# The memory's key and value units alternate between two PSUM banks, and every fourth step VectorE makes the turned weights' low halves ahead of the row maxima

## The reference, cut to what matters

```python
# differential attention, 4 heads, query blocks of 128, causal
s1 = jnp.einsum('bhqd,bhkd->bhqk', qblk[:, :, 0], k1)
s2 = jnp.einsum('bhqd,bhkd->bhqk', qblk[:, :, 1], k2)
p1 = jax.nn.softmax(jnp.where(causal, s1, NEG_INF), axis=-1)
p2 = jax.nn.softmax(jnp.where(causal, s2, NEG_INF), axis=-1)
w = p1 - lam32 * p2
out = jnp.einsum('bhqk,bhkd->bhqd', w, vh)
...
attn = rms_norm(attn, subln[i]) * (1.0 - lam_init)
...
# cross attention: the keys and values of the memory
kv = (mem_n @ wkv).reshape(b, m, 2, N_CROSS_HEADS, CROSS_HEAD_DIM)
```

## Time and profile before

| what | value |
|---|---|
| median of 3 runs | 2087.31 us |
| the profiled execution's own time | 2086.56 us |
| its span, first to last instruction | 2084.8 us |
| mean granted TensorE clock | 0.998 |
| TensorE busy | 2068.5 us (99%) |
| VectorE busy | 1651.4 us (79%) |
| ScalarE busy | 983.4 us (47%) |
| attention loop, layer 0 | from about 471 to 558 us of the span |
| attention loop, layer 1 | the same, some 1028.4 us later |

### The profile page before, as it was taken

The page is one execution under the profiler, slowest core; times in us unless marked ns, Lnnn a source line. Parts: engine busy times, 40 slices in busy tenths (PEclk is TensorE's granted clock), DMA queues, the critical chain, the costliest instruction groups (busy, mean ns, idle before and its releaser), DMA issues.

```text
span 2084.8 us, 35632 instructions
## 1 busy us (share of the span) xinstructions
PE 2068.5 (99%) x14647; PEld 1915.8 (92%) x14647; DVE 1651.4 (79%) x2459; ACT 983.4 (47%) x1483; POOL 149.1 (7%) x112
## 2 busy tenths in 40 slices
PE   9999999999999999999999999999999999999998
PEld 7999998889888889999989999988888888999997
DVE  7998886659754889988799988766696457898885
ACT  6444444446533544444454444443464345444442
POOL 0000003100120300000110000030002111000001
PEclk9999999999999999999999999999999999999999
DMA  6333323323331343433233333243233224333321
GB/s 198 102 112 106 100 85 120 119 81 102 102 102 41 98 125 107 124 95 91 80 113 118 107 114 104 66 144 99 81 103 111 71 69 133 91 112 103 102 85 56
DMA packets 268028, 212.32 MB, mean 102 GB/s; under 512 B 7422, under 2 KB 234332, under 8 KB 267868
## 3 DMA queue, kind: packets, MB, share of 16 engines
q1 hardware_dynamic: 264608, 205.55, 31.7%
q10 hardware_dynamic: 3260, 4.51, 0.8%
HBM read 207.93 MB, written 2.10 MB: 101 GB/s over the span
## 4 chain that ended last, share of the span: by engine, by line
PE 93%; DVE 5%; ACT 2%; issue 0%; ACTq 0%; DVEq 0%
PE ps L2116 18%; PE ps L1989 13%; PE ps L1991 13%; PE ps L1990 13%; PE ps L2217 11%; PE ps L2216 11%; PE ps L2218 11%; DVE nb L1837 1%; DVE w_lo L1193 1%; ACT ex L1075 1%; DVE ex L1857 1%; DVE ps L1835 0%; PE ps L2367 0%; PE ps L2558 0%; PE ps L2003 0%
## 5 line engine op out<-in xcount | busy, mean ns | idle before, releaser
L2116 PE MATMUL ps<-hid_hi,wn_hi 128*128 128x256 f32 x1088 | 212.0, 276 | 0.0
L2116 PE MATMUL ps<-hid_hi,wn_lo 128*128 128x256 f32 x1088 | 211.8, 276 | 0.0
L2116 PE MATMUL ps<-hid_lo,wn_hi 128*128 128x256 f32 x1088 | 211.8, 276 | 0.0
L1452 DVE SCALAR_TENSOR_TENSOR h<-ps,h 128x512 f32<-128x512 f32 x224 | 152.7, 683 | 30.3 <-PE ps L2116 26.8
L663 ACT ACTIVATE w_hi<-raw 128x2048 fp32r<-128x2048 f32 x61 | 117.0, 1918 | 123.0 <-PE ps L1991 90.9
L2116 PEld LDWEIGHTS ps<-hid_hi,wn_hi 128*128 128x128 f32 x1088 | 163.9, 188 | 0.0
L2116 PEld LDWEIGHTS ps<-hid_hi,wn_lo 128*128 128x128 f32 x1088 | 163.7, 188 | 0.0
L2116 PEld LDWEIGHTS ps<-hid_lo,wn_hi 128*128 128x128 f32 x1088 | 163.7, 188 | 0.0
L2216 PE MATMUL ps<-hn_hi,form_hi 128*128 128x256 f32 x576 | 159.0, 276 | 0.0
L2218 PE MATMUL ps<-hn_hi,form_lo 128*128 128x256 f32 x576 | 159.0, 276 | 0.0
L2217 PE MATMUL ps<-hn_lo,form_hi 128*128 128x256 f32 x576 | 159.0, 276 | 0.0
(11 more groups left out here) (339 smaller groups left out, 6122.3 us busy)
## 6 DMA issues: line engine op xcount, KB each, us to landing
sraw<-in_ffn_wgu_dram SPq DMA_DIRECT2D x144, 512.0 KB, 4.9
raw<-in_ffn_wd_dram SPq DMA_DIRECT2D x48, 512.0 KB, 3.8
raw<-in_ffn_wd_dram SPq DMA_DIRECT2D x80, 256.0 KB, 4.0
raw<-in_w_in_dram SPq DMA_DIRECT2D x40, 512.0 KB, 4.5
raw<-in_cross_wkv_dram SPq DMA_DIRECT2D x32, 512.0 KB, 4.3
raw<-in_ffn_wgu_dram SPq DMA_DIRECT2D x30, 512.0 KB, 4.8
raw<-in_w_out_dram SPq DMA_DIRECT2D x16, 512.0 KB, 4.2
raw<-in_cross_wq_dram SPq DMA_DIRECT2D x16, 512.0 KB, 3.8
```

The costliest lines, as they stand in the source:

```text
L1452: dve.scalar_tensor_tensor(out=h[:, m, :], in0=ps[:, down_bank(c, m), :], scalar=0.5, in1=h[:, m, :], op0=ALU.mult, op1=ALU.add).then_inc( ...
L2116: last = pe.matmul(ps[:, bank, c], w, src[:, b, c], start=opens, stop=stop and n == 2, skip_group_check=half == 1)
```

## The change

`kv_bank` becomes one function for all engines and puts units 2, 4 and 6 into bank 3, next to `head_norm`. TensorE's waits follow: unit n from 3 on waits for the low half of unit n - 2 (for unit 3 of unit 0), unit 2 for the last of the value tiles that was in bank 3, units 4 and 6 also for ACT's copy of bank 3 for head 0 and head 1. `head_norm` part 1 waits for the low half of the unit that was in bank 3 before it. On DVE `turned_low(s - 1)` moves ahead of `maxima(s)` at s = 3, 7, 11 and 15; the other steps keep their order.

```diff
+        def kv_bank(n):
+            return 1 if n == 1 else 3 if n in (2, 4, 6) else 2
+
...
-                def kv_bank(n):
-                    return 1 if n == 1 else 2
...
+                    if s < 16 and s % 4 == 3:
+                        turned_low(s - 1)
                     if s < 16:
                         maxima(s)
                     if s == 0:
                         gate_chunk(3)
-                    if 2 <= s < 17 and s % 4 != 1:
+                    if 2 <= s < 17 and s % 2 == 0:
                         turned_low(s - 1)
...
                 if part == 1:
                     pe.wait_ge(osq_ready, L * 4 + hd + 1)
+                    pe.wait_ge(kv_ready, L * 8 + min(2 * hd + 3, 8))
...
                 def cross_kv(s):
                     n, c = s // 2, s % 2
                     if c == 0:
                         wait_unit(L, CK + n)
-                        if n >= 2:
-                            pe.wait_ge(kv_ready, L * 8 + (1 if n == 2 else n))
+                        if n >= 3:
+                            pe.wait_ge(kv_ready, L * 8 + (1 if n == 3 else n - 1))
                         else:
                             pe.wait_ge(v_ready, L * 4 + kv_bank(n) + 1)
+                        if n in (4, 6):
+                            pe.wait_ge(orb_ready, L * 4 + n // 2 - 1)
```

## The result

The changed kernel takes **2102.61 us** (median of six runs, 2098.10 to 2105.88) against 2087.34 for the kernel before (six runs, 2087.25 to 2087.45): ratio 1.0069, 95% interval 1.0059 to 1.0079. It is slower, as forecast, but by 15.3 us and not by 8.6, and its time lies above the range. The spread matters too: 7.8 us from run to run, where the kernel before had 0.2 in its six runs here and up to 2.7 in the 21 runs beside each group of experiments.

What follows compares the result with a forecast made beforehand. TensorE held 93% of the chain, but DVE and ACT set the pace in the attention loops' ring. Two layers at 4.3 us added 8.6 to the profiled 2086.56, the median 0.75 more: 2095.9 us, range 2089.9 to 2098.7.

Steps and rivals of the forecast that it cites:

- Part 1: DVE's reorder at steps 3, 7, 11 and 15: maxima and exponentials come 0.33 us later each time.
- Part 2: Units 4 and 6 in bank 3 wait for ACT's late copy; with the reorders, 4.3 us more per layer.
- Part 3: The other edits, including unit 2, unit 3, head_norm and new wait instructions: put at nothing, at worst 1.2 us for the instructions.
- the 2.57: Delay of unit 4's start, 509.31 instead of 506.74, with the first 0.33 us reorder included.
- the stands: TensorE standing still before units 4 and 6, waiting for ACT's copy: some 2.8 us, four times in all.
- rival 3: Slower still, 5%: clock falls to 1.2 GHz after each stall, four times 2.8, 11.2 us more, 2107 us.
- the lower bound: If DVE made up its delay between the copies: 2.57 + 0.33 a layer, 5.8 in all, 2093.1 us.
- The 0.88 of the earlier trace: Granted clock, of 2.4 GHz, in the 7 us at the kernel's end where TensorE runs out of work.
- Rivals 1 and 2: First, 4%: waits go, nothing replaces them, 2084.4 us. Second, 6%: stall off the path, only reorders count, 2089.9 us.

Runs made afterwards that it cites:

- order_only: Kernel before with only VectorE's new order (turned_low ahead of maxima), banks and waits as before: 2090.07 us, ratio 1.0015.
- copy_early: Changed kernel with ACT's copy of bank 3 ahead of its 1.93 us rounding of a weight unit: 2090.04 us, ratio 1.0014.
- copy_late: Changed kernel with ACT's copy of bank 3 one place later, behind the exponentials of the next step: 2109.52 us, ratio 1.0104.
- bank_copy_early: Changed kernel with VectorE's old order and ACT's copy of bank 3 ahead of its weight-unit rounding: 2087.55 us, ratio 0.9999.
- again: Changed kernel run once more with no edit: 2101.51 us, ratio 1.0066.
- bank_only: Kernel before with only the change's banks and their waits, VectorE's order as before: 2097.42 us, ratio 1.0054.
- wait_only: Kernel before with one added wait, units 4 and 6 for ACT's copy, though they stay in bank 2: 2100.07 us, ratio 1.0053.
- low_late: bank_copy_early with VectorE making the step's weights before the unit's low half: 2084.89 us, ratio 0.9986.
- low_late_old_banks: low_late without the exchange of banks, all units except 1 in bank 2 with the waits of before: 2086.77 us, ratio 0.9998.

## Why the prediction was right in part, and wrong in its time

**Part 1, the reorder, held.** 0.33 us in each of steps 3, 7, 11 and 15 was forecast; order_only measures 1.35 us a layer. At step 3 the score of step 5 starts at 489.26 - 1.81 (the late start) = 487.45; 487.43 was forecast.

**Part 2, the wait for ACT's copy, held.** Unit 4 starts at 511.17 - 1.81 = 509.36; the forecast was 509.31. The forecast of 4.3 us a layer stands against some 4.45 at full clock, worked out from the loops. Bank 3's later reader is ACT's copy, and copy_early and copy_late move the cost down and up with it alone. Part 3, nothing for the other edits, is borne out by bank_copy_early at 2087.55. One slip in the bounds changes nothing: behind the 2.57 two reorders are left in a layer, 0.66 and not 0.33, so the lower bound would be 2093.8 and not 2093.1.

**What failed is a term of the sum put at nothing: the clock behind the stands.** The prediction worked out the length of the stand, 2.8 us, and named the fall of the clock as rival 3, but gave it 5%, since "no row here shows one", and let TensorE run at full clock behind it. In the four profiles that have a gap of 2.66 to 2.91 us the clock fell at 13 of 16 places (three of four here, four in again, two in bank_only, four in wait_only), and after a gap of 4.21 us at four of four. One fall cost 515.59 - 511.17 - 2.80 = 1.62 us in the first place, 1.64 between the two layers and 1.64 in bank_only; where the slow stretch lasted about twice as long, it cost 2.79, which is the price that rival 3 put down for each. Three falls of the short kind are some 5 us, and two layers at 4.45 make 8.9: 2087.3 + 13.9 = 2101.2, inside the measured spread and 1.4 below the median, whose own rows are not known. The profile's remaining 1.8 are the start.

The row that rival 3 draws on was also read too coarsely. The 0.88 of the earlier trace rows is a mean of the two levels: in the kernel before the clock is full up to 2075 and at 1.2 GHz behind that, up to the end of the span.

```profile
2073.00:2075.00 2.00, 2.00 (x21) 2.00 (x19) 0.11 (x1) 0.00 (x0) 0.00 (x0) 1.00 0.00 0
2075.40:2077.40 2.00, 1.62 (x8) 1.22 (x7) 0.43 (x2) 0.28 (x1) 1.02 (x1) 0.50 0.00 0
```

TensorE was still at work when it fell: it had waited 0.85 us for VectorE before the transposes at 2072.76 (a gap of 1.12 from start to start), and had then made transposes and sixteen matmuls of one column each. So the trace of before held a fall behind a wait much shorter than 2.8 us. The work around it is unlike that of the loop, so it gave no chance for the four stands; but it was no reason for as little as 5%.

The page "TensorE: Matmul & The Clock Gate" of the Trainium skill, section "Part 1: The HAM clock gate", says that the idle array's clock is halved; the rows at 0.50 behind the stands agree, and the second place of the changed kernel's profile, at 1.00, shows that here it is not certain for a stand of this length.

**Rivals 1 and 2 are out.** The copy did not end before TensorE was there. The stall was not hidden: VectorE waits 2.88 us at `turned_low(8)` behind a fall of the clock, and still 1.30 us in layer 1 of bank_only, where the clock held, and that loop is 3.2 us longer. The advice of the Trainium skill, page "Perfetto Trace Analysis", section "Matmuls", to rotate banks proved worth something only in low_late: 74.19 against 75.2 us a loop with the old banks. There the gap before unit 4 is 0.86 us for ACT's copy, against 1.36 for the late low half.

## What to carry to other kernels

Before a tile moves to another bank, look up who reads that bank last and where that reading stands in its engine's queue; a short copy behind a long rounding is late by the whole rounding, and moving it one place was worth 12 us here. In a ring of engines, move ahead what the ring waits for and let the rest fill the waits: the same kind of swap cost 2.7 us where it put the maxima back, and gained 2.7 us where it brought the weights forward with the banks exchanged and the copy early; with the old banks that swap gained nothing that could be measured. And when a sum contains a new stand of TensorE, price the clock behind it as a likely term, not as a remote rival.

## What the runs showed of the hardware that was not expected

After gaps of 2.66 to 2.91 us between the starts of two matmuls the granted clock fell to 1.2 GHz at 13 of 16 places, and the same place of the same kernel fell in one profile and not in the other (533.60 in the changed kernel, full clock; its counterpart at 532 in again, 0.50). Each fall cost about 1.6 us, or 2.8 where the slow stretch lasted about twice as long. That makes a program with such stands scatter by some 7 us between executions (6.3 in bank_only, 3.7 in wait_only) where the kernel before scattered by 0.2 to 2.7. In the three kernels whose longest gap in the loop is 1.42 or 1.43 us (order_only, copy_early, low_late_old_banks) no stretch of matmuls in the loop runs at half speed, and the loops of the two layers agree to 0.07 us.

The length of the gap alone does not decide. At the start of the kernel the clock stayed full behind a gap of 2.4 us in the changed kernel (13.9) and of 2.5 in order_only and bank_only, and fell behind one of 2.1 in copy_late; and in the kernel before it fell at 2075.3 with TensorE still at work, behind a gap of 1.12 us and matmuls of one column. What in the work around a gap decides is not shown. The window in copy_late right behind its gap of 2.1 us:

```profile
14.50:17.00 2.50, 2.50 (x8) 1.91 (x7) 2.46 (x5) 2.48 (x5) 0.00 (x0) 0.50 1.09 316
```

The first score of layer 0 comes between 470.75 and 472.76 us in the twelve profiles, whatever the kernel. Where it comes early TensorE had waited 0.9 us for ACT's rounding of the first weights, where it comes late up to 2.2 (copy_late, the latest, had 1.8 and the fall at the start); and in the changed kernel that rounding itself waited 1.16 us for their DMA. A difference of 1.8 us between two spans is therefore not evidence; the loop's length, the same to 0.08 us between the two layers of one profile wherever the clock held, is.
